# Output projection of the second block: four attention halves ahead of the SSM halves, in four PSUM banks

## The reference

```python
q, k, v, z_att, z_ssm, xbc, dt_raw = jnp.split(x @ w_in, SPLITS, axis=-1)
...                                              # dilated attention -> y_att, state space scan -> y
y_att = rms_norm_2(y_att * jax.nn.silu(z_att), att_norm_g)
y_ssm = rms_norm_2(y * jax.nn.silu(z_ssm), ssm_norm_g)
out = jnp.concatenate([y_att, y_ssm], axis=-1) @ w_out      # 2048 -> 1024
x = layer_norm(alpha * x + out, ln_g, ln_b)
```

## Time and profile before

| | us |
|---|---|
| median of 3 runs | 1461.89 (1459.84 to 1462.93) |
| profiled execution, its own time | 1460.57 |
| its span | 1458.6 |
| TensorE busy | 1303.0 (89%) |
| VectorE, ScalarE, GpSimd busy | 592.3, 436.2, 202.9 |

### The profile page before, as it was taken

One profiled execution on the slowest core, in us unless ns is written; L12 is line 12 of the kernel. 1 busy time (PEld: TensorE's weight loads), 2 busy tenths in 40 slices (PEclk: granted clock), 3 DMA queues, 4 the chain that ended last, 5 costly groups with the idle time before them and its releaser, 6 DMA issues.

```text
span 1458.6 us, 17705 instructions
## 1 busy us (share of the span) xinstructions
PE 1303.0 (89%) x7000; PEld 910.0 (62%) x7000; DVE 592.3 (41%) x1063; ACT 436.2 (30%) x807; POOL 202.9 (14%) x160
## 2 busy tenths in 40 slices
PE   5899989999998999999883599999899788997995
PEld 2577546788876554444441388976578666774773
DVE  0554565634432532111101552235557364337224
ACT  2332246522222311111111422235633223234112
POOL 0300010000000000000002325014020553227000
PEclk9899999999999899999997699999999699999998
DMA  9564231033332699999997033220023001321201
GB/s 334 187 237 168 87 145 59 16 92 96 102 114 92 250 386 412 411 412 412 411 397 257 20 94 95 89 71 1 2 72 102 1 0 30 87 87 44 87 15 58
DMA packets 61776, 219.88 MB, mean 151 GB/s; under 512 B 6384, under 2 KB 6776, under 8 KB 61696
## 3 DMA queue, kind: packets, MB, share of 16 engines
q1 hardware_dynamic: 55440, 198.86, 37.8%
q10 hardware_dynamic: 3952, 11.52, 2.0%
q0 software_dynamic: 2304, 8.39, 1.5%
HBM read 203.52 MB, written 15.22 MB: 150 GB/s over the span
## 4 chain that ended last, share of the span: by engine, by line
PE 75%; DMA 7%; DVE 6%; POOL 4%; issue 4%; ACT 3%; SPq 0%; ACTq 0%; POOLq 0%; DVEq 0%
PE ps L565 12%; PE ps L566 11%; PE ps L567 11%; PE ps L832 6%; PE ps L812 4%; PE ps L854 3%; PE ps L637 3%; PE ps L660 3%; PE ps L597 2%; PE ps L647 2%; DMA ring<-in_w_moe 2%; DMA ring<-in_w_pre 2%; PE ps L588 2%; PE ps L590 2%; PE ps L589 2%
## 5 line engine op out<-in xcount | busy, mean ns | idle before, releaser
L1382 DVE TENSOR_TENSOR ring_r<-ring,ring_r 128x1024 fp32r<-128x1024 f32 x116 | 150.0, 1300 | 228.1 <-ACT ring_r L1122 226.8
L565 PE MATMUL ps<-RB_r,ring_r 128*128 128x512 f32 x352 | 141.3, 401 | 21.6 <-DVE RA L1775 13.4
L1122 ACT ACTIVATE ring_r<-ring 128x1024 fp32r<-128x1024 f32 x116 | 120.0, 1052 | 135.1 <-PE ps L567 120.4
L567 PE MATMUL ps<-RB_r,ring_r 128*128 128x512 f32 x352 | 138.8, 394 | 0.0
L566 PE MATMUL ps<-RG_r,ring_r 128*128 128x512 f32 x352 | 138.3, 393 | 0.0
L565 PE MATMUL ps<-RC_r,ring_r 128*128 128x512 f32 x224 | 93.4, 417 | 5.0 <-POOL RD_r L2021 4.7
L565 PEld LDWEIGHTS ps<-RB_r,ring_r 128*128 128x128 f32 x352 | 67.2, 191 | 40.7 <-DVE RA L1775 14.2
L567 PE MATMUL ps<-RC_r,ring_r 128*128 128x512 f32 x224 | 87.5, 390 | 0.0
L2014 POOL DMA_INDIRECT RC<-expert_rows,small x4 | 3.8, 962 | 592.7 <-POOLq L2009 591.8
L566 PEld LDWEIGHTS ps<-RG_r,ring_r 128*128 128x128 f32 x352 | 66.7, 190 | 16.7 <-issue 3.6
L567 PEld LDWEIGHTS ps<-RB_r,ring_r 128*128 128x128 f32 x352 | 67.2, 191 | 14.5
(11 more groups left out here) (385 smaller groups left out, 2572.0 us busy)
## 6 DMA issues: line engine op xcount, KB each, us to landing
ring<-in_w_moe SPq DMA_DIRECT2D x120, 512.0 KB, 15.6
ring<-in_w_post SPq DMA_DIRECT2D x68, 512.0 KB, 3.6
ring<-in_w_pre SPq DMA_DIRECT2D x48, 512.0 KB, 3.6
RE<-in_w_moe SPq DMA_DIRECT2D x44, 512.0 KB, 15.6
RF<-in_w_moe SPq DMA_DIRECT2D x40, 512.0 KB, 16.1
ring<-in_w_pre SPq DMA_DIRECT2D x16, 1024.0 KB, 7.1
expert_rows<-RD ACTq DMA_DIRECT2D x17, 512.0 KB, 6.8
ring<-in_w_pre SPq DMA_DIRECT2D x4, 2048.0 KB, 18.2
```

What stands on the lines that cost most here:

```text
L565: mm(out, part(m)[:, w], xh(k), start=first and k == 0, stop=False)
L567: ins = mm(out, remainder(m)[:, w], xh(k), start=False, stop=last and k == n_k - 1)
L1122: A(part(m), tile, ACT.Copy).then_inc(w_hi, 1)
L1382: v.tensor_tensor(remainder(m), arrival(m)[2], part(m).bitcast(F32), ALU.subtract).then_inc(w_split, 1)
```

## The change

- TensorE: the order of the 16 halves becomes `OUT_ORDER`: the attention halves of tiles 0 to 3, their SSM halves, then tiles 4 to 7 with both halves of each in turn. Tile i lies in bank 6, 7, 0 or 1 (`out_bank`), and before the first half TensorE waits for both banks 6 and 7 to be free. The mean of tile i - 1 follows tile i's second half, as before.
- Weight tiles are loaded from their old places in HBM in the new order (`stored_post`), and `used` follows it.
- ScalarE: the attention root stands behind Silu 10, the copies to RD behind Silu 12. The weight copies `hi` of the third and fourth half stand ahead of the SSM root.
- VectorE: the attention norm is in step 11. The weight remainders `lo` of the third and fourth half stand ahead of the SSM norm; later ones are made up to the half two behind tile i's second one, ahead of tile i's sum.
- GpSimd: RE remainders 0 to 3 stand behind product 13, 4 to 7 behind product 14.

```diff
--- before.py
+++ after.py
@@ -39,6 +39,8 @@
 MAX_OVER = 8
 EXP_PAIRS, QUADS = N_EXP // 2, N_EXP // 4
 MOE_SLOTS = 20
+OUT_AHEAD = 4
+OUT_ORDER = [(i, s) for s in range(2) for i in range(OUT_AHEAD)] + [(i, s) for i in range(OUT_AHEAD, KT) for s in range(2)]
 ALPHA = 2.0 ** 0.25
 SSM_H, SSM_P = 16, 64
 
@@ -340,6 +342,13 @@
 
             return 16 + 3 * m if m < M_G else 67 + m - M_G
 
+        def stored_post(n):
+
+            if n < M_OUT - M_Q2:
+                return n
+            i, s = OUT_ORDER[n - (M_OUT - M_Q2)]
+            return M_OUT - M_Q2 + 2 * i + s
+
         def arrival(m):
 
             if m < M_Q2:
@@ -359,8 +368,8 @@
                 if first <= m < M_OUT:
                     return acc, e + m - first + 1
             if m >= M_OUT:
-                i = (m - M_OUT) // 2
-                return (acc, PE_OUT + i + 1) if m % 2 else (half_used, i + 1)
+                i, s = OUT_ORDER[m - M_OUT]
+                return (acc, PE_OUT + i + 1) if s else (half_used, i + 1)
             return (acc, PE_S1 + m + 1) if m < M_G else (g_used, m - M_G + 1)
 
         M_V, M_V2 = M_S1 + 12, M_Q2 + 16
@@ -416,6 +425,9 @@
         def bank(e):
             return ps[6 + e % 2]
 
+
+        def out_bank(i):
+            return ps[(6, 7, 0, 1)[i % 4]]
 
         def half(ap, h):
             return ap[(h % 2) * 64:(h % 2) * 64 + 64, h // 2, :]
@@ -528,7 +540,7 @@
                     sp.wait_ge(moe_used, N_STATIC + n_over * PAIR_TILES)
                 else:
                     sp.wait_ge(*used(M_Q2 + n - RING))
-                sp.dma_start(ring[:, n % RING, :], post_d[n]).then_inc(arrival(M_Q2 + n)[0], 16)
+                sp.dma_start(ring[:, n % RING, :], post_d[stored_post(n)]).then_inc(arrival(M_Q2 + n)[0], 16)
             for k in range(KT):
                 sp.wait_ge(fin_ok, k + 1)
                 sp.dma_start(out_d[k * P:(k + 1) * P, :], RC[:, k, :]).then_inc(out_done, 16)
@@ -1014,15 +1026,26 @@
                 pe.wait_ge(r_ok, k + 1)
                 return mm(ps[4][:, :], ones[:, :], RA[:, k, :], start=(k == 0), stop=(k == KT - 1))
 
-            for i in range(KT):
-                e = PE_OUT + i
-                free_bank(e)
-                for s, x in ((0, two(RDr, REr)), (1, two(RFr, RCr))):
-                    last = split_tile(bank(e)[:, :], M_OUT + 2 * i + s, x, first=(s == 0), last=(s == 1),
-                                      ready=(lambda k: (x_lo, 24 + KT * s + k + 1)) if i == 0 else None)
-                    last.then_inc(*((acc, 1) if s else (half_used, 1)))
+            def out_half(m, x, first, last, signal, ready=None):
+                i = OUT_ORDER[m - M_OUT][0]
+                split_tile(out_bank(i)[:, :], m, x, first=first, last=last, ready=ready).then_inc(signal, 1)
+
+            att, ssm = two(RDr, REr), two(RFr, RCr)
+            free_bank(PE_OUT)
+            free_bank(PE_OUT + 1)
+            for i in range(OUT_AHEAD):
+                out_half(M_OUT + i, att, True, False, half_used,
+                         ready=(lambda k: (x_lo, 24 + k + 1)) if i == 0 else None)
+            for i in range(OUT_AHEAD):
+                out_half(M_OUT + OUT_AHEAD + i, ssm, False, True, acc,
+                         ready=(lambda k: (x_lo, 24 + KT + k + 1)) if i == 0 else None)
                 if i:
                     mean(i - 1)
+            for i in range(OUT_AHEAD, KT):
+                pe.wait_ge(ev[i % 2], (PE_OUT + i) // 2 - 1)
+                out_half(M_OUT + 2 * i, att, True, False, half_used)
+                out_half(M_OUT + 2 * i + 1, ssm, False, True, acc)
+                mean(i - 1)
 
             mean(KT - 1).then_inc(mu_full, 1)
             stats(ST_VAR, KT, 5)
@@ -1347,13 +1370,15 @@
                     act.wait_ge(mixp, i - 3)
                 act.wait_ge(acc, e + 1)
                 A(zbuf(i), bank(e)[:, :], ACT.Silu).then_inc(ev[e % 2], 1)
+                if i == 10:
+                    root(5, ST_AT, KT, 2, eps2)
                 if i == 12:
-                    root(5, ST_AT, KT, 2, eps2)
-                if i == 14:
                     mix_parts(RDr, RB, 0)
+            hi(M_OUT + 2)
+            hi(M_OUT + 3)
             root(6, ST_SS, KT, 3, eps2)
             mix_parts(RFr, RH, KT)
-            for m in range(M_OUT + 2, M_OUT + 2 * KT):
+            for m in range(M_OUT + 4, M_OUT + 2 * KT):
                 hi(m)
             norm(7, ST_VAR, KT, 5, lambda k: RC[:, k, :], lambda k: act.wait_ge(cen_ok, k + 1), eps2)
 
@@ -1925,17 +1950,20 @@
                 lo(M_Z + i + 2)
                 if i:
                     mix_square(i - 1)
-                if i == 13:
+                if i == 11:
                     mix_norm(6, RB, "att_g")
             mix_square(15)
+            lo(M_OUT + 2)
+            lo(M_OUT + 3)
             mix_norm(7, RH, "ssm_g")
+            split = 4
             for i in range(KT):
                 e = PE_OUT + i
-                if i + 1 < KT:
-                    lo(M_OUT + 2 * i + 2)
-                    lo(M_OUT + 2 * i + 3)
+                while split < min(2 * KT, OUT_ORDER.index((i, 1)) + 3):
+                    lo(M_OUT + split)
+                    split += 1
                 dve.wait_ge(acc, e + 1)
-                v.scalar_tensor_tensor(RA[:, i, :], RA[:, i, :], ALPHA, bank(e)[:, :], ALU.mult,
+                v.scalar_tensor_tensor(RA[:, i, :], RA[:, i, :], ALPHA, out_bank(i)[:, :], ALU.mult,
                                        ALU.add).then_inc(r_ok, 1)
                 dve.wait_ge(r_ok, i + 1)
                 dve.sem_inc(ev[e % 2], 1)
@@ -2064,7 +2092,8 @@
                 tile = RB[:, i, :] if i < KT else RH[:, i - KT, :]
                 pool.wait_ge(ev[e % 2], e // 2 + 1)
                 g.tensor_tensor(tile, tile, zbuf(i), ALU.mult).then_inc(mixp, 1)
-            remainders(REr, RDr, RB, 32, range(KT))
+                if i in (13, 14):
+                    remainders(REr, RDr, RB, 32, range(4 * (i - 13), 4 * (i - 12)))
             remainders(RCr, RFr, RH, 40, range(KT))
 
 
```

## The result

| | before | after |
|---|---|---|
| median, first comparison | 1461.89 us (1459.18 to 1463.59, 5 runs) | 1452.46 us (1451.0 to 1455.51, 5 runs) |
| ratio | | 0.994, interval 0.9922 to 0.9958 |
| profiled execution, its time and span | 1460.57, 1458.6 | 1455.51, 1453.5 |
| silu 15 (start) to the end of the span | 136.7 | 127.8 |

The change makes the kernel 0.6% faster, 9.4 us between the medians.

What follows compares the result with a forecast made beforehand. TensorE was taken to wait in the output stage for GpSimd's RE and RC remainders. Hiding these gains 13.1 us, less 1.7 for a late square 15: 11.4 us below the median 1461.89, so 1450.5 us, range 1447.2 to 1455.2.

Steps and rivals of the forecast that it cites:

- rival A: TensorE's clock falls in a 4.1 us idle time before square 15, losing 1.7 us: 1452.2 us; chance 0.28.
- What was to be had, 13.1 us: Output stage: without waits behind square 15, TensorE reaches the first mean at 1348.77 instead of 1361.90 us.
- SSM chain hidden behind four halves: Four attention halves (21.8 us) before the first SSM half cover its norm and remainders, at least 3.6 us over.
- Two extra splits free: VectorE: two weight remainders before the SSM norms take 2.5 us while the root takes 3.8 us, costing nothing.
- Weight order, banks, attention norm sooner: Reordered weight loads, idle banks 0 and 1, and attention norm two columns sooner were each to cost nothing.
- Square 15 late by 1.7 us: GpSimd: RE remainders before products 14 and 15 delay square 15, summed step by step to 1327.74 us.
- rival C: VectorE and GpSimd block each other for whole instructions: square 15 ready at 1329.05, 3.1 us late, 1451.8 us; chance 0.07.
- The clock: TensorE keeps full clock through the idle time before square 15, between dense matmuls, losing nothing; forecast's chance 0.42.
- B: VectorE's splits fall between GpSimd's operations: 12.5 to 14.6 us gained, 1447.3 to 1449.4 us; chance 0.13.
- D: GpSimd at its upper bound, square 15 4.6 us late, plus the clock loss: 6.8 us gained, 1455.1 us; chance 0.05.
- E: Late weight loads on ScalarE hold up the SSM norm, making the kernel slower, about 1465 us; chance 0.03.
- F: The first SSM half still waits for the norm because GpSimd can't keep up: 1452 to 1460 us; chance 0.02.

Runs made afterwards that it cites:

- e2: Changed kernel with GpSimd's RE remainders 4 to 7 behind product 15 instead of in front of it; median 1449.97 us, ratio 0.9912 to before.
- e1: Changed kernel with fourteen extra matmuls, result overwritten, between the statistics of squares 14 and 15; median 1454.23 us, ratio 0.9945 to before.
- e6: Changed kernel with two attention halves ahead instead of four; profiled only: silu 15 to the end 128.86 us against 127.80.
- e7: As e3, but the weight splits of the third and fourth half behind the SSM norm; profiled only: silu 15 to the end 134.11 us.
- e3: Changed kernel with attention root, norm, copies and RE remainders back at their old places, only the order of halves new; median 1454.81 us, ratio 0.9945.
- e8: The changed kernel itself, profiled and timed again; median 1454.12 us, ratio 0.9939 to before.
- e4: Kernel before with only the attention norm two columns sooner and its remainders between GpSimd's products; median 1458.84 us, ratio 0.9971.
- e5: Changed kernel with the statistics of square 15 behind the first attention half instead of in front of it; median 1445.72 us, ratio 0.9884 to before.

## Why the prediction was right or wrong

The measured 1452.46 us lie in the range, 2.0 above the forecast of 1450.5 and 0.3 from rival A's 1452.2.

- **What was to be had, 13.1 us.** Borne out. The distance before, less 13.1 and the 0.4 us of e2's sooner square, is 123.2; e2 without its fall is 123.3. e1, whose profile has no fall, gives it without that correction: its square is 1.6 us later than before, and 136.7 - 13.1 + 1.6 is 125.2, where 125.4 was measured.
- **SSM chain hidden behind four halves.** Right: no wait on RC in the changed kernel; with two halves fewer (e6) it is back.
- **Two extra splits free.** Right in the changed kernel (2.35 us between square 15 and the norm) and necessary (e7). Without the sooner remainders they are not free (e3).
- **Weight order, banks, attention norm sooner.** Costless as forecast: no wait on a weight tile or a bank, and columns 11 to 15 follow each other at 6.35 us.
- **Square 15 late by 1.7 us.** The step-by-step sum holds in each part: 6.46 us for remainders 0 to 3 (6.46 forecast), 2.27 for product 14 (2.26), 5.42 for remainders 4 to 7 (5.49), 1.25 for product 15 (1.29). Square 15 came 1.54 us late. e2, which takes the last four out of the way, gets 1.9 us back.
- **Whole instruction blocking (rival C).** Fell. It wanted square 15 ready at 1329.05; it was ready at 1327.54. An operation beside a split costs GpSimd 0.98 us (product 14, 2.27 against 1.29), not 1.23. The Trainium skill, SBUF — State Buffer, section "SBUF: two separate sides", has the loser blocked for the whole instruction; the runs agree that the two engines exclude each other, and show a quarter of a microsecond less.
- **The clock.** This is the step that failed in the profiles. The forecast took the clock as kept (0.42) over a fall (0.28), on the ground that the hole stands between dense matmuls. Both profiles of the changed kernel show the fall, the starts of the matmuls show what it costs, and e1's profile agrees. Rival A had mechanism and place right and the size too small: it took 1.7 us from a stretch of 3.4 us of lower level; here the lower level lasted some 6.8 us, 5.3 of them under work, 2.7 us. That the median lies only 0.3 us from A's time is luck: by the distances A's gain of 9.7 us is 0.8 too large, and it is made of a square 0.2 us too late and a fall 1.0 us too cheap.

So the account is 13.1 - 1.5 - 2.7 = 8.9 us, which is the 8.9 of the distances. The medians give 9.4, within their spread. By the medians the forecast is 2.0 us off; in the profiles it is 2.5 (11.4 forecast, 8.9 found), which is the clock's 2.7 less the 0.2 by which square 15 was sooner than forecast.

The Trainium skill, TensorE: Matmul & The Clock Gate, Part 1, ties the lower clock to an idle engine; this case agrees for the 4.1 us of the changed kernel; in e3 the fall came behind two short idle times, 0.5 and 1.8 us.

The other rivals: B fell (the splits do meet GpSimd), D fell too (square 15 was 1.54 us late and not 4.6), E and F found no trace: TensorE never waits in the SSM half.

What stays open: in how many of the untraced runs the clock falls, and with it whether the timed runs carry the 2.7 us, which e1's don't show; and why it fell in e3 and e7 but not in the kernel before, behind the same two idle times.

## What to carry to other kernels

When filler work is put into a helper engine's gaps, look at what waits for the very next item of that engine's list: four remainders in front of product 15 cost 1.5 us of lateness, and the idle time so made cost another 2.7 through the clock. An idle TensorE in front of a small dependent operation (here two matmuls of statistics) can be filled with the big work that follows it: exchanging the two was worth 6 us in the profile here. When an order is changed, list which weights each of the new steps needs, and when they are ready; in e7 a wait for one such weight tile and the clock fall behind it cost 6.4 us, as much as the order alone had gained.

## What the runs showed of the hardware that was not expected

- The granted clock fell after 2.15 us of idle time (e2) and after 0.5 and 1.8 us (e3, e7), while the kernel before, with the same 0.5 and 1.8 us at the same place, kept 1.00. The same idle time may thus be followed by either level; a single profile is no proof that a gap is harmless.
- After 4.1 us of idle time the lower level lasted about 6.8 us in three profiles (changed, e6, e8), but only 3.4 us in e4, as in e2 after 2.15 us. The same idle time thus has no fixed price either.
- With fourteen useless matmuls in the idle time the output stage was 2.4 us shorter in the one profile taken (e1).
- Eight SSM norms on VectorE took 10.6 us in the changed kernel and in e5, where GpSimd had finished with RE, and 13.33 in the kernel before, where it was still at RE during the first of them.
